# 64x64 tiles for the triangular inverse, with fills of nine wide products in its first four levels

## The reference, cut to what matters

```
x = x + 0.5 * swiglu(rms_norm(x, w1), gate1, up1, down1)
h = rms_norm(x, w_mix) @ w_in          # attention q k v | pool | delta q k v z | gates
y = concat(dilated_attention(...), multiscale_pool(...), gated_deltanet(...))
x = x + y @ w_out
x = x + 0.5 * swiglu(rms_norm(x, w2), gate2, up2, down2)
```

```
A = where(strict, (beta * k) @ k.T * decay, 0)
T = inverse(eye + A)
u = T @ (beta * v);  w = T @ (beta * k * exp(g))
```

## Time and profile before

| | |
|---|---|
| median of 3 runs | 1062.14 us (1060.95 to 1063.49) |
| profiled execution | 1065.3 us, its span 1063.5 us |
| mean granted TensorE clock | 0.985 |
| TensorE busy | 1034.6 us, 97% |
| VectorE busy | 737.6 us, 69% |
| ScalarE busy | 606.6 us, 57% |
| Pool busy | 229.3 us, 22% |

### The profile page before, as it was taken

The page is one execution under the profiler, slowest core; times in us unless marked ns, Lnnn a source line. Parts: engine busy times, 40 slices in busy tenths (PEclk is TensorE's granted clock), DMA queues, the critical chain, the costliest instruction groups (busy, mean ns, idle before and its releaser), DMA issues.

```text
span 1063.5 us, 20023 instructions
## 1 busy us (share of the span) xinstructions
PE 1034.6 (97%) x6999; PEld 894.5 (84%) x6999; DVE 737.6 (69%) x1200; ACT 606.6 (57%) x1070; POOL 229.3 (22%) x258
## 2 busy tenths in 40 slices
PE   7999999999999999999999999999999999999997
PEld 5888888889887888888888888888988778888885
DVE  5766666798666766666686666669985767666665
ACT  5655555767544655555575555558673555555554
POOL 2311111088400221111122111112013003111111
PEclk9999999999979999999999999999998899999999
DMA  8866665594123476666647666665822237666661
GB/s 255 252 192 189 187 194 170 143 235 140 58 65 100 137 219 179 197 194 182 195 126 220 189 187 194 191 180 136 208 93 63 62 117 211 186 197 194 181 197 39
DMA packets 252045, 176.94 MB, mean 166 GB/s; under 512 B 7939, under 2 KB 237592, under 8 KB 251864
## 3 DMA queue, kind: packets, MB, share of 16 engines
q1 hardware_dynamic: 250880, 174.41, 56.6%
q0 software_dynamic: 336, 1.31, 0.4%
q10 hardware_dynamic: 776, 0.49, 0.2%
HBM read 175.14 MB, written 1.05 MB: 166 GB/s over the span
## 4 chain that ended last, share of the span: by engine, by line
PE 87%; DVE 6%; ACT 3%; issue 2%; POOL 1%; DMA 1%; SPq 0%; DVEq 0%; POOLq 0%; ACTq 0%
PE bank L695 27%; PE bank L698 14%; PE bank L677 11%; PE bank L678 11%; PE bank L679 11%; DVE Wl L1778 2%; PE bank L704 1%; DVE X L1815 1%; DMA raw<-in_ffn_w_gate 1%; PE bank L1036 1%; PE bank L985 1%; PE bank L936 1%; DVE xr L1987 1%; DVE early L2025 1%; ACT X L1395 1%
## 5 line engine op out<-in xcount | busy, mean ns | idle before, releaser
L1778 DVE TENSOR_TENSOR Wl<-raw,Wh 128x1024 fp32r<-128x1024 f32 x328 | 420.0, 1287 | 81.8 <-ACT Wh L1326 81.4
L1326 ACT ACTIVATE Wh<-raw 128x1024 fp32r<-128x1024 f32 x328 | 335.5, 1054 | 78.3 <-PE bank L679 75.6
L695 PE MATMUL bank<-X,Wh 128*128 128x512 f32 x1344 | 334.7, 391 | 0.0
L695 PEld LDWEIGHTS bank<-X,Wh 128*128 128x128 f32 x1344 | 246.7, 188 | 47.6
L591 POOL TENSOR_TENSOR gact<-gact,pooled 128x256 f32<-128x256 f32 x88 | 79.5, 904 | 612.6 <-DVE gact L1871 462.2
L698 PEld LDWEIGHTS bank<-X,Wl 128*128 128x128 f32 x1344 | 183.0, 190 | 14.2 <-DVE Wl L1778 1.4
L698 PE MATMUL bank<-X,Wl 128*128 128x256 f32 x1344 | 187.8, 283 | 0.0
L677 PE MATMUL bank<-Wh,aH 128*128 128x512 f32 x336 | 132.3, 394 | 1.0 <-DVE aL L1892 1.0
L678 PE MATMUL bank<-Wl,aH 128*128 128x512 f32 x336 | 131.7, 392 | 0.0
L679 PE MATMUL bank<-Wh,aL 128*128 128x512 f32 x336 | 130.7, 389 | 0.0
L1432 ACT ACTIVATE dec<-bank 128x256 f32<-128x256 f32 x88 | 33.7, 383 | 122.3 <-PE bank L698 122.2
(11 more groups left out here) (283 smaller groups left out, 1303.0 us busy)
## 6 DMA issues: line engine op xcount, KB each, us to landing
raw<-in_ffn_w_gate SPq DMA_DIRECT2D x88, 512.0 KB, 3.9
raw<-in_ffn_w_up SPq DMA_DIRECT2D x88, 512.0 KB, 3.8
raw<-in_ffn_w_down SPq DMA_DIRECT2D x88, 512.0 KB, 4.4
raw<-in_w_in SPq DMA_DIRECT2D x48, 512.0 KB, 4.5
raw<-in_w_out SPq DMA_DIRECT2D x16, 512.0 KB, 3.7
cst<-in_consts POOLq DMA_DIRECT2D x1, 1140.0 KB, 6.0
xr<-in_x SPq DMA_DIRECT2D x2, 512.0 KB, 4.5
out_x<-big SPq DMA_DIRECT2D x3, 256.0 KB, 2.0
```

The costliest lines, as they stand in the source:

```text
L695: nc.tensor.matmul(b[:, :], piece(Wh, s)[:, k, :], X[:, k, :, :], start=k == 0, stop=False)
L1326: return nc.scalar.activation(Wh[:, s, :], raw[:, s, :], ACT.Copy).then_inc(hi_cast.sem, 1)
L1778: return nc.vector.tensor_tensor(Wl[:, s, :], raw[:, s, :], Wh[:, s, :].bitcast(F32), ALU.subtract).then_inc(lo_cast.sem, 1)
```

## The change

- The inverse's levels work on `D64` and `T64`, two 64x64 blocks per unit instead of four 32x32. The masks are 64 columns wide. The quarter and half levels take their operands from these tiles, so `Dm` goes away; `DT` is cleared on its left half alone and filled (`dt_joined`, twice) after the half level's multiplies.
- z piece 3 is taken out of the stretch ahead of the inverse. Its 24 products and the 48 of the late attention are dealt out nine at a time to the eight fills of the four levels (`fill`). Late attention now uses high and low weights in one go. The quarter and half levels have no fill, as before.
- ScalarE: `z_silu(3)` after level 1, the table load after level 2, the cast of piece 28 after the levels. At the mixer's start the fifth `copy_half` comes before the casts of pieces 8 and 9, and on VectorE the gate rows come before the casts of 10 and 11.
- The kernel's entry: the FFN1 norms are loaded first and transposed alone, the other norms later with the parameters. All splits come before the first low casts, the first four before the first high cast. The first gate and up products run over all eight blocks, high weights for both first and then low weights for both. The first hidden product comes before the low cast of the down piece.

```diff
+Z_LEVELS = 2
 N_LEVELS = len(LEVELS) + 2
-BLOCK = 32
-QUARTERS = [slice(BLOCK * i, BLOCK * (i + 1)) for i in range(P // BLOCK)]
-EVEN = BLOCK // 2
 HALF = P // 2
+BLOCKS = [slice(0, HALF), slice(HALF, P)]
+QUARTER = P // 4
+QUARTERS = [slice(QUARTER * i, QUARTER * (i + 1)) for i in range(4)]
+EVEN = HALF // 2
...
+                def wide(b, s, blocks, wait=False):
+                    pe.wait_ge(*hi_cast.at(layer, base + s + 1))
+                    for j in blocks:
                         k = SPLIT_ORDER[j]
                         if wait:
                             block_ready(layer, n, j)
                         nc.tensor.matmul(b[:, :], piece(Wh, s)[:, k, :], X[:, k, :, :], start=j == 0, stop=False,
                                          skip_group_check=True)
-                    if i == 0:
-                        pe.wait_ge(*lo_cast.at(layer, base + s + 1))
-                    for j in range(4 * i, 4 * i + 4):
+
+                def low(b, s, blocks):
+                    pe.wait_ge(*lo_cast.at(layer, base + s + 1))
+                    for j in blocks:
                         k = SPLIT_ORDER[j]
                         m = nc.tensor.matmul(b[:, SEQ:], piece(Wl, s)[:, k, :], Xh[:, k, :], start=False, stop=j == KT - 1,
                                              skip_group_check=True)
                     return m
 
-                pe.wait_ge(*gsum_done.at(layer, T - 1))
-                half(gbank[0], 0, 0, True)
-                between()
-                pe.wait_ge(*mul_done.at(layer, T - 1))
-                half(ubank[0], 1, 0)
-                half(gbank[0], 0, 1, True).then_inc(gates_done.sem, 1)
-                half(ubank[0], 1, 1).then_inc(ups_done.sem, 1)
+                whole, left, right = range(KT), range(4), range(4, KT)
+                if between is None:
+                    wide(gbank[0], 0, whole, True)
+                    wide(ubank[0], 1, whole)
+                    low(gbank[0], 0, whole).then_inc(gates_done.sem, 1)
+                    low(ubank[0], 1, whole).then_inc(ups_done.sem, 1)
...
-                for h in (2, 3):
-                    split(POS_Z + h)
-                    pe.wait_ge(*diff_done.at(layer, h - 1))
-                    column_piece(bank[h][:, 0:SEQ], MIX_SLOTS[POS_Z + h]).then_inc(proj.sem, 1)
+                split(POS_Z + 2)
+                pe.wait_ge(*diff_done.at(layer, 1))
+                column_piece(bank[2][:, 0:SEQ], MIX_SLOTS[POS_Z + 2]).then_inc(proj.sem, 1)
...
+                def z_part(ks):
+
+                    s = MIX_SLOTS[POS_Z + 3]
+                    split(POS_Z + 3)
+                    pe.wait_ge(*diff_done.at(layer, 2))
+                    for k in ks:
+                        m = three(bank[3][:, 0:SEQ], piece(Wh, s)[:, k, :], piece(Wl, s)[:, k, :], Xh[:, k, :], Xl[:, k, :],
+                                  k == 0, k == KT - 1)
+                    if ks[-1] == KT - 1:
+                        m.then_inc(proj.sem, 1)
+
+                def att_late(j, ks):
+
+                    s0, s1, t = MIX_SLOTS[POS_LATE], MIX_SLOTS[POS_LATE + 1], slice((j % 2) * P, (j % 2 + 1) * P)
+                    pair = slice(s0, s1 + 1, s1 - s0)
+                    out = bank[ATT_BANKS[j]][:, 0:2 * P].rearrange("p (s c) -> p s c", s=2)
+                    split(POS_LATE + 1)
                     pe.wait_ge(*z_act.at(layer, j - ATT_EARLY + 3))
                     for k in ks:
-                        w = Wh[:, pair, k * P:(k + 1) * P]
-                        nc.tensor.matmul(out, Xh[:, k, t], w, start=k == 0, stop=False)
-                        nc.tensor.matmul(out, Xl[:, k, t], w, start=False, stop=False)
-
-                def late_low(j, ks):
-
-                    out, t, pair = late_of(j)
-                    split(POS_LATE + 1)
-                    for k in ks:
-                        m = nc.tensor.matmul(out, Xh[:, k, t], Wl[:, pair, k * P:(k + 1) * P], start=False, stop=k == KT - 1)
-                    return m
+                        w = slice(k * P, (k + 1) * P)
+                        m = three(out, Xh[:, k, t], Xl[:, k, t], Wh[:, pair, w], Wl[:, pair, w], k == 0, k == KT - 1)
+                    if ks[-1] == KT - 1:
+                        m.then_inc(att_in.sem, 1)
...
-                        for q in QUARTERS:
-                            even = D32[q, u, :].rearrange("p (n a s) -> p n a s", a=2, s=LEVELS[n])[:, :, 0, :]
+                        for q in BLOCKS:
+                            even = D64[q, u, :].rearrange("p (n a s) -> p n a s", a=2, s=LEVELS[n])[:, :, 0, :]
                             m = nc.tensor.matmul(bank[4 + c][q, h * EVEN:(h + 1) * EVEN], LT[q, u, q], even,
...
                 def half_p(c):
 
                     pe.wait_ge(*d_done.at(layer, 8 + c + 1))
-                    pe.wait_ge(*dm_joined.at(layer, 1))
                     for h, u in units(c):
                         m = nc.tensor.matmul(bank[4 + c][HALF:, h * HALF:(h + 1) * HALF], LT[0:HALF, u, HALF:],
-                                             Dm[0:HALF, u, 0:HALF], start=True, stop=True)
+                                             D64[0:HALF, u, :], start=True, stop=True)
                     m.then_inc(p_done.sem, 1)
...
+                def fill(first):
+
+                    for i in range(first, first + 3):
+                        if i < KT:
+                            z_part(range(i, i + 1))
+                        else:
+                            att_late(6 + (i - KT) // KT, range(i % KT, i % KT + 1))
 
                 for n in range(len(LEVELS)):
                     for c in range(HALVES):
                         level_p(n, c)
-                    if n < 2:
-                        late_high(ATT_EARLY + n, range(0, 4))
-                    else:
-                        late_low(ATT_EARLY + n - 2, range(0, 4))
+                    fill(6 * n)
                     for c in range(HALVES):
                         level_d(n, c)
-                    if n < 2:
-                        late_high(ATT_EARLY + n, range(4, 8))
-                    else:
-                        late_low(ATT_EARLY + n - 2, range(4, 8)).then_inc(att_in.sem, 1)
+                    fill(6 * n + 3)
...
+                pe.wait_ge(*dt_joined.at(layer, 1))
...
                 if first:
                     for c, b in ROW_ORDER[0:2]:
                         square(c, b)
-                    hi_first(layer, 0, 0)
                     act.wait_ge(zeroed.sem, 2)
                     act.wait_ge(*turned.at(layer, 2))
                     for j in range(4):
                         split(j)
-                    hi_first(layer, 0, 1)
+                    hi_first(layer, 0, 0)
                 else:
                     act.wait_ge(*turned.at(layer, 4 * n + 2))
                     for j in range(4):
...
                 for j in range(4, 8):
                     split(j)
                 if first:
+                    hi_first(layer, 0, 1)
...
                 copy_half(3)
+                copy_half(4)
                 hi_mix(layer, 8)
                 hi_mix(layer, 9)
-                copy_half(4)
                 copy_half(5)
...
-                    if n == 0:
-                        hi_mix(layer, 28)
-                    if n == 1:
+                    if n == Z_LEVELS - 1:
+                        z_silu(3)
+                    if n == Z_LEVELS:
                         act.preload_act_table_set(LN_EXP)
-                act.wait_ge(*cleared.at(layer, 1))
-                act.wait_ge(*d_done.at(layer, 8))
-                nc.scalar.activation(Dm[QUARTERS[0], :, QUARTERS[0]], D32[QUARTERS[0], :, :], ACT.Copy)
-                nc.scalar.activation(Dm[QUARTERS[1], :, QUARTERS[1]], D32[QUARTERS[1], :, :],
-                                     ACT.Copy).then_inc(dm_joined.sem, 1)
+                hi_mix(layer, 28)
...
+            act.dma_start(nrm_first, ffn1_norm.rearrange("l (k c) -> (l k) c", c=P)).then_inc(norm_first_in.sem, 16)
             act.dma_start(cst[:, 0:C_FIRST], consts[:, 0:C_FIRST]).then_inc(consts_in.sem, 16)
-            for n, weight in enumerate((ffn1_norm, mix_norm, ffn2_norm)):
-                act.dma_start(nrm_rows[n * DEPTH * KT:(n + 1) * DEPTH * KT, :],
+            for n, weight in enumerate((mix_norm, ffn2_norm)):
+                act.dma_start(nrm_rest[n * DEPTH * KT:(n + 1) * DEPTH * KT, :],
                               weight.rearrange("l (k c) -> (l k) c", c=P)).then_inc(norms_in.sem, 16)
...
+                    nc.vector.tensor_copy(nrm_all[:, 0, :, :].rearrange("p l k -> p (l k)"),
+                                          bank[7][:, 0:DEPTH * KT]).then_inc(zeroed.sem, 1)
                     dve.wait_ge(zeroed.sem, 2)
-                    split(0)
-                    split(1)
+                    for j in range(8):
+                        split(j)
                     lo_piece(layer, 0, 0)
-                    split(2)
-                    split(3)
                     lo_piece(layer, 1, 1)
```

(72 more changed lines are left out.)

72 lines of the change are left out of this document (31 added, 41 removed).

## The result

The changed kernel took 1078.97 us (median of 16 runs, 1066.4 to 1080.64), the kernel before 1063.38 us (16 runs, 1060.89 to 1066.2) on the same chips: a ratio of 1.0119, 95% interval 1.0089 to 1.0149. The forecast was 1048.2 us with a range of 1041 to 1057. The change made the kernel slower by 1.2%, and 1048.2 was 31 us off.

What follows compares the result with a forecast made beforehand. TensorE, busy 97% of the span, was taken as the bound, with idle, slow or costly stretches in four places. Gains summing to 13.9 us took 1065.3 to 1051.4, less 3.2 for the median: 1048.2 us, range 1041 to 1057.

Steps and rivals of the forecast that it cites:

- new wait: Level 1's first fill: TensorE waits for the low cast of piece 24, a 1.2 us stall (ends 0.8 and 1.6).
- C: Rival: clock falls in level 1's wait and stays low, 7.5 us a layer, 1063.2 us, no change; chance 0.06.
- Burst of 0.5 us: Inverse levels: one step's 32 products of 64x64 for both halves take 0.5 us, ends 0.33 and 0.9.
- rival B: Rival: the levels' bursts take 0.9 us, 3.2 us less gain a layer, 1054.6 us; chance 0.20.
- No hole in the levels: Inverse levels: with half the instructions, no "issue" hole inside a run of products; before, layer 0 had one of 2.37 us.
- The clock through the levels: Inverse: granted clock expected at 1.00 through all four levels.
- late fall: Half level until past the scores: clock low for some 4.4 us, costing 2.2 us a layer, ends 0 and 3.1.
- Quarter and half levels: Quarter products to first scores: 6.1 us at full clock against 9.2; gain 0.9 us a layer after the clock's fall.
- rival A: Rival: the clock doesn't fall at all, 2.2 us more gain a layer, 1043.8 us; chance 0.17.
- Nine-fill: Inverse levels: eight fills of nine wide products, 1.26 us each, cover handovers; the 2.88 us z piece in front goes.
- Mixer's start: Mixer's start: both TensorE waits, 1.9 us, go; VectorE takes part back; gain 1.0 us a layer, ends 0 and 1.9.
- Entry: Kernel's entry: first down product at about 25.3, 1.7 us earlier, ends 0 and 3; identity's load later by 0.45 us.

Runs made afterwards that it cites:

- e9: e1 plus a TensorE wait in level 1 for an otherwise unused VectorE sum over 1664 columns (stall 1.34 us): 1079.09 us.
- e10: e1 plus a TensorE wait in level 1 for an otherwise unused VectorE sum over 1024 columns (stall 0.67 us): 1055.45 us.
- e5: The changed kernel with only the low cast of piece 24 moved, to between VectorE's two multiplies of level 1: 1053.37 us.
- e1: The changed kernel with the low casts of pieces 23 to 26 one place earlier on VectorE: 1052.12 us, ratio 0.9902 to the kernel before.
- e4: e1 with each level's first burst streaming 16 columns a product instead of 32, half the product left out: one execution of 1054.81 us.
- e2: The kernel before with all of the change but the tiles (32x32 kept, late cast kept): 1064.34 us, ratio 0.9995.
- e3: The kernel before with only the change's entry and mixer's start, inverse untouched: 1061.63 us, ratio 0.9972.
- e6: e2 (32x32 tiles, fills of nine) with the early casts of e1: 1060.23 us, ratio 0.9969 to the kernel before.
- e7: The changed kernel with z piece 3 ahead of the inverse again and the old fills of 8, 8, 4 and 4: 1054.74 us.
- e11: e1 with the identity and constants loaded ahead of the FFN norms again, as in the kernel before: 1050.69 us, ratio 0.9874.
- e8: The changed kernel unaltered, run once more for another profiled execution: 1068.12 us.

## Why the prediction was wrong, point by point

The step that failed is the price of the new wait: "1.2 us stall (ends 0.8 and 1.6)". Its place and its cause were right, and its length nearly (1.55 us, inside the ends). It was booked at its own length, but what it costs is its length and the clock. The forecast had a rival for just that (C), gave it 0.06 on the ground that there are "dense products on both sides", and that ground did not hold: six wide products stand right before the wait and three right behind it, and the clock fell all the same. The forecast had itself named, for C, the falls behind holes of 2.37 and 1.42 us. e9 and e10 show the price by a stall alone, e5 by moving the one cast.

C's own price was too low as well. Here are the terms for both layers, forecast against the profiled executions of the changed kernel and of e1 (us gained; the spans before, after and in e1 are 1063.5, 1078.6 and 1050.3):

| term | forecast | changed | e1 |
|---|---|---|---|
| four levels, with z piece 3 | 8.4 | -19.3 | 1.9 |
| quarter products to first scores | 1.8 | -0.2 | 6.5 |
| mixer's start, and the rest behind the scores | 2.0 | 3.9 | 4.2 |
| entry | 1.7 | 0.5 | 0.5 |
| sum | 13.9 | -15.1 | 13.2 |

Each entry is a difference of starting times, rounded for itself. The levels of layer 0, for one: 16.86 + 2.88 - 29.20 = -9.46 for the changed kernel, and 16.86 + 2.88 - 18.56 = 1.18 for e1.

- **Burst of 0.5 us: mis-sized.** It is 1.06 us; 8 x (1.06 + 1.26) = 18.56 us is e1's levels exactly, 4.5 more than the 14.1 of the sum. The upper end of my bounds was 0.9, rival B. I had gone by the quarter level's row, but its tiles load 32 columns each, and these load 64. In e1 the first 22 products of a burst are recorded at 0.83 us and all 32 at 1.12, 29 ns for each further one. The forecast took 0.5 us against the rule that it cites. The Trainium skill, "TensorE: Matmul & The Clock Gate", section "LDWEIGHTS (loading the stationary operand)", has a load's time in ns as its columns divided by 1.2; as an estimate from that, 64 columns are 53 ns, or 27 ns a product with two tiles side by side. The trace's 29 ns agrees with the rule, and so does e4, where halved streamed columns change nothing.
- **The wait in level 1: place right, length 1.55 for 1.2, consequence missed.** The cast takes 2.08 us and not 1.22, 0.86 more, but it starts 0.40 us behind the burst (281.52 to 281.92) and not 0.8. GpSimd rotates q and k at that time, and in the kernel before too: there a level's cast kept its 1.22 us and GpSimd's product beside it was recorded at 2.36 us, here GpSimd's was first and took 1.28 (281.64 to 282.92). The cast then ended 1.08 us after it. That one of the two waits for the other fits both rows, as an estimate; no run moved them apart.
- **No hole in the levels: right.** Neither the changed kernel nor e1 has an "issue" hole there; e2, e3 and e6 with 64 products a burst all have them. That those holes are code that arrives late is still only argued.
- **The clock through the levels.** Forecast at 1.00; it fell in level 1. From there to the quarter products the changed kernel takes 5 x (4.07 - 2.32) = 8.7 us more, and the end 3.35 us more than e1 (9.27 against 5.92). Together with the wait and the edges of the fall it makes 14.0 us a layer (10.64 + 3.35), 28.0 of the 28.3 us between the two spans. C said 6.6 for the levels, with fills 0.94 us longer, which is right (2.21 against 1.26 us), and bursts 0.5 us longer, which is 0.8 (286.55 - 284.70 = 1.85 against 1.06 us); and 0.9 for the end, on top of the late fall that the forecast had booked already. In C's sum that came to no change; measured, it is a loss.
- **Quarter and half levels.** At full clock 6.1 forecast, 5.92 measured in e1: right. The late fall priced at 2.2 us happens in some executions (8.42 us in layer 1 of e4, 8.47 in layer 1 of e7, 7.49 in layer 0 of e10) and not in others. So I booked as certain what comes now and then: as far as this stretch goes rival A held in both layers of e1, e5 and e11.
- **Nine-fill.** It gives nothing by itself: e7's z piece and levels take 2.88 + 15.67 = 18.55 us, e1's 18.56. The 72 wide products are only dealt out otherwise, and fills of four already covered the handovers.
- **Mixer's start.** Forecast 1.0 a layer. In layer 0 the levels start 1.26 us earlier, beyond z piece and entry. It would be more without the new 1.03 us wait for GpSimd. From the first scores of layer 0 to the levels of layer 1 it is 2.3 us beyond the z piece, both waits of 0.9 us in full. I had looked for the return on VectorE; it came from GpSimd, and in one layer only.
- **Entry: mis-sized.** The identity came 1.55 us later than before, not the 0.45 us of one issue, and the transposes, the splits and the first cast all stand behind it. With the old order (e11) the first down product starts at 25.19; the forecast said 25.3. The rest of that chain was right.

That e1 gained 13.2 us in its profile where the forecast had 13.9 is partly accident. Without the wait my levels would have given 10.8, 8.9 too much; the quarter and half levels gave 4.7 more than forecast, mixer's start and rest 2.2 more, and the entry 1.2 less.

The range left out the case that came. The trace of before had shown a fall of the clock behind a hole twice; by that, C deserved more than 0.06.

## What to carry to other kernels

When a change puts a wait among small-tile products, price it with the clock too: here 1.34 to 1.55 us cost 13 to 14 us a layer, and moving one VectorE cast ahead of one multiply gave nearly all of it back. Look at what follows the wait as well: the clock stayed low for some 3.4 us among wide products and 10 us among bursts of 32x32 tiles (one case each, in e2), but for about 30 us among those of 64x64. Price a small product by the size of its tile, here the columns of its weight load, not by those it streams. A load that is issued behind another can land later by more than one issue; look what the engine's very first instruction waits for.

## What the runs showed of the hardware

- The same kernel with the same wait lost the clock for the inverse in one layer (e8's profile) or in both (the changed kernel's), in steps rather than by degrees: the 16 runs have nothing between 1069.4 and 1076.8 us. Once at 0.50 it stayed there for about 30 us, although TensorE was recorded busy without a gap; it rose in 314 to 316, after eight q/k transposes (310.69) and eight products of full size (312.46). Bursts and fills that hold a clock of 1.00 in e1 did not bring it back. In e2's layer 1, with 32x32 tiles and the same fills, it was back after some 10 us.
- The stalls at one place in level 1: 0.31 us (e5) and 0.67 us (e10), clock held through the levels in both layers; 1.34 (e9) and 1.55 (changed), clock lost, but for one layer of e8 with 1.54.
- The low cast of 128x1024 takes 1.20 to 1.22 us alone. Beside GpSimd's rotation of q and k it took between 1.22 us (before, with GpSimd's product at 2.36 and not 1.27) and 2.33 (e7); in the changed kernel 2.08, with GpSimd's product at 1.28. The sum over 1664 columns took 1.87 us there and that over 1024 took 1.20.
- Changing only the order of two loads on one queue moved the first transposes, which wait for one of them, from 6.47 (e1) to 5.10 (e11): 1.37 us for an issue of 0.43 us.
